# Sixteen more tokens taken out of the dense expert matmuls of a decoder layer, and computed from gathered rows

## The reference

```python
    def chunk(args):
        xt, et, gt = args              # tokens, their 128 expert numbers, their 128 gates
        u = expert_down[et]
        h = jax.nn.gelu(jnp.einsum('cd,ced->ce', xt, u), approximate=False)
        vv = expert_up[et]
        return jnp.einsum('ce,ced->cd', gt * h, vv)
```

## Time and profile before

| | us |
|---|---|
| median of 3 runs | 2395.07 (2391.79 to 2395.18) |
| the profiled execution | 2393.62 |
| its span, first to last instruction | 2391.8 |
| PE busy | 2369.6, 99% of the span |
| LDWEIGHTS (weight loads of PE) busy | 2243.5, 94% |
| DVE busy | 1647.1, 69% |
| ACT busy | 1225.5, 51% |
| POOL busy | 609.1, 25% |
| stream, bytes of queue q1 | 449.89 MB |
| POOL's queue q0 | 92.27 MB |

### The profile page before, as it was taken

The page is one execution under the profiler, slowest core; times in us unless marked ns, Lnnn a source line. Parts: engine busy times, 40 slices in busy tenths (PEclk is TensorE's granted clock), DMA queues, the critical chain, the costliest instruction groups (busy, mean ns, idle before and its releaser), DMA issues.

```text
span 2391.8 us, 46059 instructions
## 1 busy us (share of the span) xinstructions
PE 2369.6 (99%) x16878; PEld 2243.5 (94%) x16878; DVE 1647.1 (69%) x2572; ACT 1225.5 (51%) x1793; POOL 609.1 (25%) x443
## 2 busy tenths in 40 slices
PE   9999999999999999999999999999999999999997
PEld 9999999999999999999999999999899999999996
DVE  5555555646666666888888887765766666677767
ACT  5444444545554444666565565444554445545544
POOL 0000000000000000477668887772011110111100
PEclk9999999999999999999999999999999999999999
DMA  7767666565545555587788989987788887788863
GB/s 277 225 217 226 219 220 212 183 193 159 162 154 176 195 193 185 168 204 201 215 257 255 261 260 290 300 221 234 256 297 297 298 288 271 277 293 308 317 225 108
DMA packets 180651, 555.87 MB, mean 232 GB/s; under 512 B 51712, under 2 KB 52400, under 8 KB 176224
## 3 DMA queue, kind: packets, MB, share of 16 engines
q1 hardware_dynamic: 123552, 449.89, 56.6%
q0 software_dynamic: 53280, 92.27, 14.2%
q10 hardware_dynamic: 3744, 12.78, 1.8%
HBM read 522.01 MB, written 31.78 MB: 232 GB/s over the span
## 4 chain that ended last, share of the span: by engine, by line
PE 97%; DVE 2%; ACT 1%; issue 0%; ACTq 0%; DVEq 0%
PE ps L1362 37%; PE ps L1629 18%; PE ps L1633 9%; PE ps L1617 9%; PE ps L1613 9%; PE ps L1616 5%; PE ps L1614 5%; PE ps L1401 1%; PE ps L1416 1%; DVE w_first L811 1%; PE ps L1431 0%; PE ps L1403 0%; PE ps L1409 0%; ACT w_first L492 0%; PE ps L1591 0%; PE ps L1417 0%
## 5 line engine op out<-in xcount | busy, mean ns | idle before, releaser
L811 DVE TENSOR_TENSOR w_first<-raw,w_first 128x1024 fp32r<-128x1024 f32 x425 | 520.1, 1224 | 366.3 <-ACT w_first L492 365.6
L811 DVE TENSOR_TENSOR w_second<-raw,w_second 128x1024 fp32r<-128x1024 f32 x425 | 520.2, 1224 | 131.5 <-ACT w_second L492 130.3
L492 ACT ACTIVATE w_second<-raw 128x1024 fp32r<-128x1024 f32 x425 | 447.8, 1054 | 190.4 <-PE ps L1629 175.4
L492 ACT ACTIVATE w_first<-raw 128x1024 fp32r<-128x1024 f32 x425 | 448.8, 1056 | 148.3 <-PE ps L1629 118.8
L434 POOL DMA_INDIRECT g_dram<-lists x256 | 443.8, 1734 | 102.0 <-issue 80.0
L1629 PE MATMUL ps<-m_two,w_first 128*128 128x480 f32 x1024 | 329.0, 380 | 1.5 <-DVE m_two L1248 1.5
L1629 PE MATMUL ps<-m_two,w_second 128*128 128x480 f32 x1024 | 327.8, 379 | 0.5 <-DVE m_two L1248 0.5
L1362 PE MATMUL ps<-a_all,w_first 128*128 128x256 f32 x2472 | 306.2, 280 | 0.0
L1362 PE MATMUL ps<-a_all,w_second 128*128 128x256 f32 x2472 | 298.3, 276 | 0.2 <-DVE a_all L842 0.2
L1362 PEld LDWEIGHTS ps<-a_all,w_first 128*128 128x128 f32 x2472 | 291.1, 188 | 1.0
L1362 PEld LDWEIGHTS ps<-a_all,w_second 128*128 128x128 f32 x2472 | 288.4, 188 | 0.4 <-DVE a_all L842 0.4
(11 more groups left out here) (271 smaller groups left out, 4002.5 us busy)
## 6 DMA issues: line engine op xcount, KB each, us to landing
raw<-stream SPq DMA_DIRECT2D x850, 512.0 KB, 3.4
sc<-g_dram POOLq DMA_DIRECT2D x43, 480.0 KB, 4.7
g_dram<-rot POOLq DMA_DIRECT2D x32, 512.0 KB, 6.2
a_dram<-act ACTq DMA_DIRECT2D x26, 480.0 KB, 3.5
more<-a_dram POOLq DMA_DIRECT2D x17, 480.0 KB, 5.5
late_a<-a_dram POOLq DMA_DIRECT2D x10, 480.0 KB, 6.0
g_dram<-lists POOLq DMA_INDIRECT x256
keep<-a_dram POOLq DMA_DIRECT2D x6, 480.0 KB, 8.8
```

The costliest lines, as they stand in the source:

```text
L492: act.activation(w_hi[t.slot(hf)], raw[:, t.slot(hf), :], ACT.Copy).then_inc(hi_ready, 1)
L811: dve.tensor_tensor(w_lo[s], raw[:, s, :], w_hi[s].bitcast(F32), ALU.subtract).then_inc(lo_ready, 1)
```

## The change

`EXTRA` = 16 further tokens (the 16 ahead of the routed ones in the same half) leave the dense work, so that `DENSE` goes from 240 to 224: products of 448 and 224 columns instead of 480 and 240, in down and in both up passes. Their rows are treated like the routed ones, in 16 more columns: the rows of `expert_down` are gathered and dotted with `h_extra` in the first up pass, one every three tiles from tile 6; their GELU and gates follow in the same pass (`EXTRA_GELU_AT`, `extra_gated`); the rows of `expert_up` are gathered and added into `e_acc` in the second pass. There, 32 columns now stand where 16 stood: two in every three tiles, from tile 67 of the passes on. Both kinds use the same two row buffers.

For that, memory is laid out anew: `KEPT` goes from 6 to 4 (two more blocks go through HBM), the product slots from 21 to 20 (12 blocks instead of 11 are multiplied again in the second pass, one every three tiles instead of every four). The scatters of the second half go over 96 tokens instead of 112. POOL issues eight more copies of 128 KB (`h_extra`) and eight more small ones (`routed_e`). `x_sums` makes twice as many products.

```diff
 ROUTED = 16
-DENSE = T - ROUTED
+EXTRA = 16
+DENSE = T - ROUTED - EXTRA
...
-KEPT, SLOTS_M, TEMPS = 6, 21, 3
+KEPT, SLOTS_M, TEMPS = 4, 20, 3
...
-MULT_AT = [2 * u - 1 for u in range(BLOCKS)] + [2 * BLOCKS + 14 + 4 * j for j in range(BLOCKS - SLOTS_M)]
-X_AT = [2 * (BLOCKS + 3) + 3 * c for c in range(COLUMNS)]
+MULT_AT = [2 * u - 1 for u in range(BLOCKS)] + [2 * BLOCKS + 14 + 3 * j for j in range(BLOCKS - SLOTS_M)]
+ROW_AT = [6 + 3 * d for d in range(EXTRA_COLS)] + [PASS + 3 + 3 * c // 2 for c in range(COLUMNS + EXTRA_COLS)]
+EXTRA_GELU_AT = ROW_AT[EXTRA_COLS - 1] + 4
...
-        def x_fetch(c):
-
-            if c >= 2:
-                pool.wait_ge(x_ready, c - 1)
-            pool.indirect_dma_start(out=row_buf[c % 2], out_offset=None, in_=up_rows,
-                                    in_offset=bass.IndirectOffsetOnAxis(ap=routed[:, 0, c:c + 1], axis=0)).then_inc(xrow_in[c % 2], 16)
+        def row_fetch(i):
+
+            if i >= 2:
+                pool.wait_ge(row_used, i - 1)
+            c = i - EXTRA_COLS
+            table, at = ((rows_dram, routed_e[:, 0, i:i + 1]) if c < 0 else (up_rows, routed[:, 0, c:c + 1]) if c < COLUMNS else
+                         (up_rows, routed_e[:, 0, c - COLUMNS:c - COLUMNS + 1]))
+            pool.indirect_dma_start(out=row_buf[i % 2], out_offset=None, in_=table,
+                                    in_offset=bass.IndirectOffsetOnAxis(ap=at, axis=0)).then_inc(xrow_in[i % 2], 16)
...
+        for g in range(EXTRA_GROUPS):
+            pool.dma_start(h_extra[EXTRA * g:EXTRA * g + EXTRA, :], h1_row[EXTRA_AT:ROUTED_AT, :]).then_inc(rows_in, 16)
...
-            n = ROUTED_AT if tt else P
+            n = EXTRA_AT if tt else P
...
+            pool.dma_start(routed_e[EXTRA * j:EXTRA * j + EXTRA], lists[EXTRA_AT:ROUTED_AT, 1, :, j, :]).then_inc(routed_in, 16)
...
+        for k in range(2, len(MULT_USES)):
+            u = MULT_USES[k]
+            at = max([at, MULT_AT[k - 2]] + [2 * v for v in range(u) if USE_SLOT[v] == USE_SLOT[u]])
+            order.append((at, 0, k))
+        order += [(ROW_AT[i - 2] if i >= 2 else 0, 1, i) for i in range(len(ROW_AT))]
+        for _, row, n in sorted(order):
+            row_fetch(n) if row else load(n)
...
+        def extra_dot(i):
+
+            row = row_in_place(i)
+            dve.scalar_tensor_tensor(out=row, in0=row, scalar=1.0, in1=h_extra[:], op0=ALU.mult, op1=ALU.mult,
+                                     accum_out=u_e[:, i:i + 1]).then_inc(row_used, 1)
...
-            pe.wait_ge(x_ready, COLUMNS)
+            pe.wait_ge(row_used, len(ROW_AT))
             for c in range(8):
-                for k, o in ((c, 480), (c + 8, 496)):
-                    ins = pe.matmul(bank[c][:, o:o + ROUTED], x_acc[:, P * k:P * k + P], small[:, S_SEL:S_SEL + ROUTED],
+                for k, o in ((c, 2 * DENSE), (c + 8, 2 * DENSE + EXTRA + ROUTED)):
+                    pe.matmul(bank[c][:, o:o + EXTRA], e_acc[:, P * k:P * k + P], small[:, S_SEL_E:S_SEL_E + EXTRA],
+                              start=False, stop=False, skip_group_check=True)
+                    ins = pe.matmul(bank[c][:, o + EXTRA:o + EXTRA + ROUTED], x_acc[:, P * k:P * k + P], small[:, S_SEL:S_SEL + ROUTED],
```

More of the change, by code:

```diff
@@ L206, in build @@
     peer_mem = ExitStack()
+    square_mem = ExitStack()
+    r_sq = sb("r_sq", [P, 4, HALF], F32, square_mem)
+    square_mem.close()
     keep = sb("keep", [P, KEPT, 4, DENSE], F32, peer_mem)
@@ L309, in build @@
         row_mem[:, 0:8 * DENSE], sc_flat[:, 8 * DENSE:16 * DENSE])]
-    m_slot = [m[:, b] for m, n in zip([keep, late_a] + late + [more], (KEPT, 8, 2, 2, 3)) for b in range(n)]
+    m_slot = [m[:, b] for m, n in zip([keep, late_a] + late + [more], (KEPT, 9, 2, 2, 3)) for b in range(n)]
     low_s = h_rows[:, 0:8 * DENSE].rearrange("p (c t) -> p c t", c=8)
-    x_acc = h_rows
+    x_acc, e_acc = h_rows, h_extra
     qp_flat = qp.rearrange("p k t -> p (k t)")
@@ L468, in _ @@
             pool.wait_ge(a_out[b], (BLOCKS - KEPT) // 2 * 16 + 16)
-        for k in range(2, BLOCKS):
-            load(k)
         pool.wait_ge(dot_ready, COLUMNS)
[L472 to L478, removed]
+        order, at = [], 0
+        for k in range(2, len(MULT_USES)):
[5 more added lines that the diff above has]
+            row_fetch(n) if row else load(n)
     @block.scalar
@@ L779, in _ @@
                     act.activation(low_s[:, c, :], bank[c][:, DENSE:2 * DENSE], ACT.Copy).then_inc(low_out, 1)
+            if q == EXTRA_GELU_AT:
+                act.wait_ge(row_used, EXTRA_COLS)
+                act.activation(val_e[:], u_e[:], ACT.Gelu).then_inc(extra_gelu, 1)
             if q == 2 * PASS - 6:
@@ L1256, in scale_res, with row_in_place, extra_gated, row_add @@
                                      op0=ALU.mult, op1=ALU.add).then_inc(res_ready, 1)
-        def x_add(c):
-            dve.wait_ge(xrow_in[c % 2], 16 * (c // 2) + 16)
+        def row_in_place(i):
+            dve.wait_ge(xrow_in[i % 2], 16 * (i // 2) + 16)
+            return row_buf[i % 2]
+        def extra_dot(i):
+            row = row_in_place(i)
+            dve.scalar_tensor_tensor(out=row, in0=row, scalar=1.0, in1=h_extra[:], op0=ALU.mult, op1=ALU.mult,
+                                     accum_out=u_e[:, i:i + 1]).then_inc(row_used, 1)
+        def extra_gated():
+            dve.wait_ge(extra_gelu, 1)
+            dve.tensor_tensor(val_e[:], val_e[:], routed_e[:, 2, :].bitcast(F32), ALU.mult).then_inc(extra_val, 1)
+        def row_add(i, total, val, c):
+            row = row_in_place(i)
             if c == 0:
-                dve.wait_ge(vb_ready, len(GELU_COLS))
-                dve.wait_ge(low_added, 1)
-                dve.tensor_scalar(x_acc[:], row_buf[0], val_b[:, 0:1], None, ALU.mult).then_inc(x_ready, 1)
-            else:
-                dve.wait_ge(x_ready, c)
-                dve.scalar_tensor_tensor(out=x_acc[:], in0=row_buf[c % 2], scalar=val_b[:, c:c + 1], in1=x_acc[:],
-                                         op0=ALU.mult, op1=ALU.add).then_inc(x_ready, 1)
+                dve.tensor_scalar(total[:], row, val[:, 0:1], None, ALU.mult).then_inc(row_used, 1)
+            else:
+                dve.wait_ge(row_used, i)
+                dve.scalar_tensor_tensor(out=total[:], in0=row, scalar=val[:, c:c + 1], in1=total[:],
+                                         op0=ALU.mult, op1=ALU.add).then_inc(row_used, 1)
+        def row_step(i):
+            c = i - EXTRA_COLS
+            if c < 0:
+                extra_dot(i)
+            elif c < COLUMNS:
+                if c == 0:
+                    dve.wait_ge(vb_ready, len(GELU_COLS))
+                    dve.wait_ge(low_added, 1)
+                row_add(i, x_acc, val_b, c)
+            else:
+                if c == COLUMNS:
+                    dve.wait_ge(extra_val, 1)
+                row_add(i, e_acc, val_e, c - COLUMNS)
         add_low(NKEYS - 2)
@@ L1298, in _ @@
                     both = res.rearrange("p (a c) t -> p c a t", a=2)[:, c, :, DENSE:T]
-                    dve.tensor_tensor(both, bank[c][:, 480:512].rearrange("p (a t) -> p a t", a=2), both, ALU.add).then_inc(x_out, 1)
+                    dve.tensor_tensor(both, bank[c][:, 2 * DENSE:512].rearrange("p (a t) -> p a t", a=2), both, ALU.add).then_inc(x_out, 1)
             if q == 2 * PASS - 6:
```

38 lines of the change are left out of this document (24 added, 14 removed).

## The result

The changed kernel takes 2382.24 us (median of 5 runs, 2376.12 to 2382.86), the kernel before 2394.12 (now a median of 5). The ratio is 0.9948, 95% interval 0.9936 to 0.9959: 0.5% faster. Forecast were 2347 us and a range of 2322 to 2370. The sign was right, the size was not: 12 us were gained of 47.

The account below looks back on a forecast made before the run. PE was taken to bound the kernel, its instructions one behind the other. Span 2391.8 - 59.4 + 4.5 + 1 + 6 = 2343.9, with 1.8 around it and 1.45 for the runs' median: 2347 us, range 2322 to 2370.

Parts of the forecast that it names:

- Removed on PE: Down and up passes: wide products save 14.5 ns each, narrow ones nothing; -59.4 us over 256 tiles.
- the first rival: Down and up: the narrow product does follow its columns, PE saves 89 us, 2322 us in all; chance 12%.
- Added on PE: `x_sums`: 32 more instructions cost 3.5 us and the lower clock behind them 1 us; +4.5 us.
- POOL and the scatters: Down: later copies shrink the cover before the first `m_mult` from 52.7 to 15.4 us; no cost.
- The DMAs: Up passes: demand of 369 GB/s in the first, 409 in the second, ceiling 411 to 416; +1 and +6 us.
- The second rival: Up passes: the DMAs bound the second and part of the first; at 361 GB/s, 2369 us; chance 20%.
- The fourth rival: Second up pass: DVE bounds it through gaps of 0.1 us at each instruction; 2352 to 2360 us; chance 10%.
- Slower by late gathers: Up passes: gathers land after their turn, holding up DVE and PE; 3.6 us a round gives 2400 us; chance 4%.

Follow-up runs that it names:

- 128-column run: The kernel before, with the narrow product in down at 128 columns instead of 240, the rest of the low-part product left out: 2397.32 us.

## Why the prediction was wrong, step by step

The steps that failed are the terms for what is given back. I had 7 us for the DMAs in the up passes, 0 for the copies on POOL and 1 for the clock, 8 in all. The traces show 24.1, 10.2 and 4.9, or 39. The saving on PE came out 4.8 us smaller.

- **Removed on PE: mechanism right, 4.8 us too large.** -59.4 forecast, -54.6 measured. The wide product saves 13.4 ns, at its lower bound of 13.3, not 14.5. The narrow one saves nothing, as argued: its starts are still 0.11 us apart, and the 128-column run gains nothing. That refutes the first rival (it follows its columns).
- **Added on PE: half right.** 32 more instructions cost 3.5 us, but the clock cost 4.9 more, where I had 1 (bounds 0 to 3.5). I priced a stretch of low work twice as long by the low clock behind the shorter one. The clock stayed low for 13.7 us instead of 3.4. This execution is one of the dearest: where the low clock lasted 6.8 us, the block cost 5.1 us more than before, 1.6 above the 3.5 of its instructions, which is near the 1 I took.
- **POOL and the scatters: the cover held, the step failed.** The gates were in time. The eight copies were costed by what they take on POOL's list, 3.8 us, and not as traffic of the DMAs. They and the old eight held the DMAs for some 12 us at 126 to 148 GB/s, and the stream behind them. That is 10.2 us on a step I set to none. The earlier trace rows showed the issue only; the window of the kernel before at that place shows 130 GB/s at a share of 1.01.
- **The DMAs: mechanism right, size wrong.** I had +6 in the second pass and +1 in the first; measured are 16.2 and 7.9. The bytes' own part is 6.0 us in the run with short adds, at 391 GB/s. My +6 agrees with it, partly by luck: I had 7.7 at 390 GB/s and 0 at 411 and called 6 "near the middle", which would be 4. What was missing is that DVE's queue and the DMAs were costed one by one, each as if the other were punctual. DVE at 92% was within its limit and the DMAs were some 0.5 us a round over theirs; together they form a loop of 17.0 us where 15.1 were at hand. The second rival's rate (361 GB/s) is what the changed kernel reached, but not for its reason: 391 were to be had. The fourth rival, DVE by itself, is refuted by the run with every other gather: DVE has all its work there, and the second pass no excess.
- **Slower by late gathers: no.** The trace shows no wait of DVE at an add or a dot for its row. In both up passes DVE waited for ACT's copies (117 us in all), and ACT for the stream.

What stays open: the first pass. Its excess of 8 us falls to 4 with half the gathers or with short dots. In tiles 3 and 4 it is 3.7 with short dots and 4.3 without the row work, but 0.2 to 1.3 with only one gather there or with both later, so the two gathers at the start have a part in it. What the two blocks more cost there was not tried, and moving the gathers shortened the pass in one of three runs. Why the low clock lasts 6.8 us in one kernel and 13.7 in another is open too.

## What to carry to other kernels

Add up an engine's work and the DMAs' bytes per round, and then look for the loop through both: who frees the buffer whose reload competes with what the same instruction releases. Here 92% of one and 100% of the other cost 16.6 us in the second pass, where either of them alone cost 0 and 6. A group of small copies between few partitions must be priced as DMA time, not by its issue or its bytes, and spread out. And the short products were cheapest one by one between long ones: 7.0 us instead of 10.3 to 13.6.

## What the runs showed of the hardware that I had not expected

- Gathers of 64 rows into 64 partitions cost the DMAs nearly as much as 128 rows into 128: POOL's queue took 16.9% of their time for 100.95 MB against 17.5% for 126.12 MB.
- Sixteen copies of 128 KB, each from 16 partitions to 16, ran beside the stream at 126 to 148 GB/s in all, at a DMA share of 0.94 to 1.06. Their packets of 8 KB took 0.94 us on average, those of late gathers 0.36.
- 7 us of 16-column products brought 6.8, 10.2 or 13.7 us at 1.2 GHz, by the execution; 3.6 us of them 3.4 us; the same products one behind each pair of long ones none.
- A float32r product that loads its own weights takes 0.11 us at 240 and at 224 columns; with 128 columns two neighbours share 0.17 us but the next long product gives it back.
